# Down projections: the second column group takes every second slab by Strassen's scheme, with three more sets of side sums where x was

## The chip, the cores and the metric

The kernel runs on one core of one Trainium2 chip. The metric is the device time of one execution in microseconds (us). Before the change it is 2428.57 us, the median of three runs (2427.8 to 2428.59).

## What is computed

Two transformer blocks in a row on 256 tokens of width 2048, all in fp32. The part that the change touches is the last product of the feed-forward network, which occurs twice (once in each layer of the second block):

```python
D_FF = 5632
def swiglu(h, w_gate, w_up, w_down):
    return (jax.nn.silu(h @ w_gate) * (h @ w_up)) @ w_down
x = x + rmsnorm(swiglu(h, w_ffn_gate[l], w_ffn_up[l], w_ffn_down[l]), norm_ffn_post[l])   # l = 0, 1
```

So per layer a 256x5632 matrix g (gated activations) is multiplied by a 5632x2048 weight matrix. To keep fp32 accuracy every operand is split into a high part (rounded to the matmul type) and a low part (the rest), and each product is made of three matmuls: hi x hi, hi x lo, lo x hi.

## The kernel before

**Slabs.** Weights come in slabs of 1 MB: 128 partitions of 2048 floats, fetched as two DMAs of 512 KB by SyncE (L688, `fetch_part`). Each slab passes from SyncE (DMA into one of 5 ring places of `raw`) to ScalarE (`conv`, L1486: the high part into one of 4 places of `hi`), to VectorE (`conv`, L2098: the low part, in place), and to TensorE. A list `slabs`, made once, gives the order; every engine goes through it in that order. SyncE may fill a place when the slab five entries back is used, ScalarE may write `hi` when the slab four entries back is used (`slab_used`).

**A down projection** (`st_down[l]`) has two column groups g = 0 and 1 of 1024 output columns, and 22 slabs s = 0 to 21 in each. A slab holds two blocks of 128 rows by two halves of 512 columns. An ordinary slab is 2 token tiles x 2 column halves x 2 row blocks = 8 products, 24 matmuls of 128x512 (`product`, L808 to L810), accumulated in the four PSUM banks `acc`.

**Strassen's scheme** (`seven`, matmuls in L1248 to L1250). For the slabs named in `SEVEN[g]` the 2x2 by 2x2 block product is made of 7 products, so 21 matmuls. It takes sums of weight blocks and sums of activation blocks:
- The sums of weights (`weight_sums`, L2160 to L2163, VectorE, 4 operations) are made anew for each group. Three of them fill a ring place of their own; they are an entry `sums{s}` of `slabs` behind the slab, with a conversion of its own of 1536 columns (128x768 twice).
- The sums of activations ("side sums": `side_sums` on VectorE, L2236 to L2241, then `side_hi` on ScalarE, L1548, then `side_lo` on VectorE, L2246) are made once in group 0 and read again in group 1, so each needs 4 KB per partition of its own until group 1 has used it. There are five such sets, for slabs 3, 6, 9, 12, 15, and both groups use the scheme for just these five.
- Four of the seven products are accumulated in the PSUM banks `wk`. After the last such slab (15) VectorE combines them (`mix_products`, L2252 to L2256, in its order ahead of the conversion of slab 18) and adds them into `acc` (`mix_into_acc`, L2263 and L2266, ahead of the conversion of slab 19). TensorE waits for the first two additions ahead of slab 17's second token tile and for the other two ahead of slab 18's first one (`acc_loaded`, with `MIX_DONE` = 16).

On VectorE and ScalarE the order is one straight program: `conv_to(m)` goes through the slabs up to m, and `before(m)` holds what VectorE does ahead of the conversion of slab m. ScalarE does `side_hi` ahead of its conversion of the slab at which the side sums are made, so that conversion waits until VectorE has made the sums.

**x.** The residual x (16 KB per partition at `X0`) is stored to HBM earlier (`keep_x`), and its place is used for sums in the gate/up stage. SyncE fetches it back (`fetch_x`, L700, two DMAs of 1 MB) ahead of the weights of slab 3 of group 0, and VectorE waits for it (`x_fetched`) at the start of the down projection. Its first reader is `add_normed`, after the down projection.

Of the kernel before, what the change touches and what calls it, by code (L numbers as in the profile page):

```python
# [13 lines left out]
D = 2048  # L14
# [14 lines left out]
FG = FF // HALF  # L29
# [7 lines left out]
TAKEN_BELOW = -3.2e38  # L37
RING = 5
OWN_SLOT = 9
SEVEN = ((3, 6, 9, 12, 15), (3, 6, 9, 12, 15))  # L40
HI_SLOTS = 4
SLAB = 2048

# [53 lines left out]
def build(nc, t_in, out):  # L97
# [22 lines left out]
    m_a = at("m_a", [P, TT, 2 * D], A0)  # L120
    gain_a = at("gain_a", [P, D], A0 + 24)

    SIDES_AT = (A0 + 8, A0 + 12, A0 + 4, A0 + 20, S0 + 1)
    side = [at(f"side{i}", [P, 2, 4, P], kb) for i, kb in enumerate(SIDES_AT)]
    side_r = [at(f"side_r{i}", [P, 2, 4, P], kb, F32R) for i, kb in enumerate(SIDES_AT)]
    CHAINED = 2
# [207 lines left out]
    def sevens(m):  # L334

        st, g, s = slabs[m]
        return st_down.index(st) if st in st_down and s in SEVEN[g] else None
# [14 lines left out]

        return (FG - CHAINED) * l + g - CHAINED

    N_SIDES = len(SEVEN[0])
    DOWN_SIDES = [6 + l * (6 + 2 * N_SIDES) for l in range(2)]
    GU_SIDES = [l * (6 + 2 * N_SIDES) for l in range(2)]
    DOWN_HIS = [4 + l * (4 + N_SIDES) for l in range(2)]
# [295 lines left out]
    @block.sync  # L654
    def _(sp):
        def const(name, dst):
            a, w = CONSTS[name]
            sp.dma_start(dst, t_in["consts"][:, a:a + w]).then_inc(consts_in, 16)

        const("ident", ident[:])  # L660
        sp.dma_start(rows2[0:KT, :], t_in["c"][0].rearrange("(k p) -> k p", p=P)).then_inc(rows_in, 16)
        sp.dma_start(rows2[KT:2 * KT, :], t_in["hgrn_lb_logits"].rearrange("a (k p) -> (a k) p", p=P)).then_inc(rows_in, 16)

        def wait_summed(a):

            if a in PE_ADA:
                sp.wait_ge(ada_taken, PE_ADA.index(a) + 1)
            else:
                sp.wait_ge(ada_added, added(a + 1))

        def ada_fetch(a, landed):

            for part in range(2):
                src, dst = ada_part(a, part)
                sp.dma_start(dst, src).then_inc(landed, 16)

        for a in range(4):
            ada_fetch(a, raw_landed[1 + a])
        def fetch_part(slot, st, g, s, part, landed):

            src, (a, b), how = st.src(g, s, part)
            if how is None:
                dst = slot[:, a:b]
            elif how == "part":
                dst = slot.rearrange("p (k h n) -> p k h n", k=2, h=2)[:, :, part, :]
            else:
                dst = slot[:, a:b].rearrange("p (k n) -> p k n", n=how)
            sp.dma_start(dst, src).then_inc(landed, 16)  # L688

        def keep_x(l):  # L690

            sp.wait_ge(x_ready, 4 * l + 2)
            for t in range(TT):
                sp.dma_start(x_kept[:, t], x[:, t]).then_inc(stored, 16)

        def fetch_x(l):

            sp.wait_ge(slab_used, number[st_gu[l].name, FG - 1, "D"] + 1)
            for t in range(TT):
                sp.dma_start(x[:, t], x_kept[:, t]).then_inc(x_fetched, 16)  # L700

        def fetch_own(l, g):

            if g == CHAINED:
                sp.wait_ge(stored, 16 * TT * (l + 1))
                sp.wait_ge(x_squares, 8 + 4 * l)
                sp.wait_ge(h_ready, h_done((3, 6)[l]) + 8)
            else:
                sp.wait_ge(slab_used, number[st_gu[l].name, g - 1, "C"] + 1)
            for part in range(2):  # L710
                fetch_part(raw[:, OWN_SLOT], st_gu[l], g, 1, part, own_landed)

        for m, (st, g, s) in enumerate(RAWS):
            if st in st_gu:
                l = st_gu.index(st)
                if (g, s) == (0, 7):
                    keep_x(l)
                if s == 7 and g + 1 in OWN_GROUPS:
                    fetch_own(l, g + 1)
            if st in st_down and (g, s) == (0, 3):  # L720
                fetch_x(st_down.index(st))
            if isinstance(s, str):
                continue
            r = m % RING
            if m == 1:
                for a in range(4, N_QUARTER):
                    ada_fetch(a, early_landed[a - 4])
            if m == 2:
                ada_fetch(8, quarter_landed[0])
                sp.wait_ge(xn_ready, 1)  # L730
                ada_fetch(9, quarter_landed[1])
            if m == 3:
                sp.wait_ge(xn_ready, 2)
                ada_fetch(10, quarter_landed[2])
                sp.wait_ge(ada_added, added(7))
                ada_fetch(11, early_landed[2])
            if m == 4:
                sp.wait_ge(ada_added, added(8))
                ada_fetch(12, early_landed[3])
            if 1 <= m < RING:  # L740
                wait_summed(m - 1)
            elif m:
                sp.wait_ge(slab_used, LAST_USE[m - RING] + 1)
            for part in range(2):
                fetch_part(raw[:, r], st, g, s, part, raw_landed[r])

        for t in range(TT):
            for half in range(2):
                c = slice(half * GW, (half + 1) * GW)
                sp.wait_ge((x_half, x_ready)[half], 6 + t + 1)  # L750
                sp.dma_start(out[0, t * P:(t + 1) * P, c], x[:, t, c]).then_inc(stored, 16)
        sp.wait_ge(stored, 16 * 4 * TT)
# [3 lines left out]
    def _(pe):  # L756
# [479 lines left out]

        def seven(l, g, s):

            st, i = st_down[l], SEVEN[0].index(s)
            m = number[st.name, g, s]  # L1240
            k0, k1 = 2 * s, 2 * s + 1
            s1, s2, s3, s4 = ((side_r[i][:, 0, j, :], side_r[i][:, 1, j, :]) for j in range(4))

            def add(o, lhs, slab, q, first=False, last=False):

                c = slice(q * HALF, (q + 1) * HALF)
                w_hi, w_lo = hi[:, slab % HI_SLOTS, c], lo[:, place(*slabs[slab]), c]
                pe.matmul(o, lhs[0], w_hi, start=first, stop=False)  # L1248
                pe.matmul(o, lhs[0], w_lo, start=False, stop=False)
                return pe.matmul(o, lhs[1], w_hi, start=False, stop=last)  # L1250

            first, last = s == min(SEVEN[g]), s == max(SEVEN[g])
            pe.wait_ge(slab_split, m + 1)
            pe.wait_ge(g_ready, 2 * FG * (l + 1) if first else 2 * FG * l + s + 1)
            add(wk[:, 0, :], gt(k0, 0), m, 0, first, last)
            add(acc[:, 0, :], gt(k1, 0), m, 2)
            pe.wait_ge(side_made, DOWN_SIDES[l] + 2 * i + 2)
            add(acc[:, 1, :], s4, m, 3)
            add(wk[:, 3, :], s3, m, 1, first, last).then_inc(slab_used, 1)
            pe.wait_ge(slab_split, m + 2)  # L1260
            add(wk[:, 1, :], s1, m + 1, 0, first, last)
            add(wk[:, 2, :], s2, m + 1, 1, first, last)
            add(acc[:, 2, :], gt(k1, 1), m + 1, 2).then_inc(slab_used, 1)
# [199 lines left out]
    def _(act):  # L1463
# [43 lines left out]
        def conv_to(m):  # L1507

            while made[0] <= min(m, N_SLABS - 1):
                if sevens(made[0]) is not None and slabs[made[0]][1] == 0:  # L1510
                    side_hi(sevens(made[0]), SEVEN[0].index(slabs[made[0]][2]))
                conv(made[0])
                st, g, s = slabs[made[0]]
                if st in st_gu and g == CHAINED - 1 and s in (5, 6, 7):
                    l = st_gu.index(st)
                    if s > 5:
                        side_hi_pair(l, s - 6)
                    if s < 7:
                        tile_hi_pair(l, s - 5)
                made[0] += 1  # L1520
# [529 lines left out]
    def _(vec):  # L2050
# [63 lines left out]
        def conv_to(m):  # L2114

            while made[0] <= min(m, N_SLABS - 1):
                ada_to(ada_until(made[0]))
                before(made[0])
                conv(made[0])
                if sevens(made[0]) is not None and slabs[made[0]][1] == 0:  # L2120
                    side_lo(sevens(made[0]), SEVEN[0].index(slabs[made[0]][2]))
                made[0] += 1

        def before(m):
# [15 lines left out]
                    third_sum(l, g)  # L2140
            if st in st_down:
                l = st_down.index(st)
                if g == 0 and s in SEVEN[0]:
                    side_sums(l, SEVEN[0].index(s))
                if s in SEVEN[g]:
                    weight_sums(m)
                if s == MIX_DONE + 2:
# [79 lines left out]

        def side_sums(l, i):

            s, gu = SEVEN[0][i], st_gu[l]  # L2230
            a11, a21, a12, a22 = (side[i][:, 0, j, :] for j in range(4))
            s1, s2, s3, s4 = (side[i][:, 1, j, :] for j in range(4))
            flat = "p k t -> p (k t)"
# [599 lines left out]
        def ffn(l):  # L2833
# [31 lines left out]
            for g in range(FG):  # L2865
# [12 lines left out]
                else:  # L2878
                    conv_to(end + 4)
                post(g)  # L2880
            vec.wait_ge(x_fetched, 16 * TT * (l + 1))
            return m_evac(st_down[l], m_a, gain_a, (post_in, 16 * (l + 1)), 1 + 2 * l)

        skewed_turn(ffn(0), m_a, 1, 4, st_k)
        row_scale(3)
# [253 lines left out]
```

## Time and profile before

| | |
|---|---|
| median of three runs | 2428.57 us |
| profiled execution, own time | 2428.43 us |
| its span, first to last instruction | 2426.6 us |
| TensorE busy | 2384.8 us, 98% |
| VectorE busy | 1973.3 us, 81% |
| ScalarE busy | 1299.3 us, 54% |
| granted TensorE clock, mean | 0.996 |
| down projection of layer 0, about | 1100 to 1333 us of the span |
| down projection of layer 1, about | 2184 to 2418 us |

How to read it: the span is the time between the first and the last instruction of one profiled execution. Matmul durations overlap (they are pipelined), so the pace is read from one start to the next. A row "[1.25 <-PE acc L1250]" says that the engine was idle for 1.25 us before the instruction and that the matmuls of line 1250 ended the wait.

### The profile page before, as it was taken

How to read it: one execution, taken by the hardware profiler on the slowest of the kernel's cores; microseconds unless marked ns; L12 is line 12 of the kernel's file. 1: busy time of each engine (PE TensorE's matmuls, PEld its weight loads, DVE VectorE, ACT ScalarE, POOL GpSimd, SP SyncE). 2: the span in 40 equal slices, each digit the busy share in tenths (PEclk: the TensorE clock that was granted, in tenths of full speed). 3: DMA queues.
4: the chain of work that ended last, by engine and by line, in shares of the span. 5: the costliest groups of instructions: out<-in, count | busy, mean ns of one | idle time of the engine just before them, and what ended most of it. 6: DMA issues, size and time to landing. Idle time of an engine off the chain costs nothing.

```text
span 2426.6 us, 28811 instructions
## 1 busy us (share of the span) xinstructions
PE 2384.8 (98%) x11030; PEld 1979.5 (82%) x11030; DVE 1973.3 (81%) x2564; ACT 1299.3 (54%) x1703; POOL 99.0 (4%) x150
## 2 busy tenths in 40 slices
PE   5999999999999999999999999999999999999998
PEld 4888878888888888888888888888888888888887
DVE  6998988766889899897777768965699898988776
ACT  4757765445555555654444544554555555555443
POOL 0210000000000000000000212100000000000000
PEclk8999999999999999999999999999999999999999
DMA  9997665474566566566656655446666565565654
GB/s 383 360 385 246 240 208 171 166 262 167 192 208 208 191 208 196 186 199 215 229 188 205 196 196 193 160 142 203 218 210 200 188 212 188 195 222 189 224 191 156
DMA packets 190649, 515.46 MB, mean 212 GB/s; under 512 B 17920, under 2 KB 18208, under 8 KB 188208
## 3 DMA queue, kind: packets, MB, share of 16 engines
q1 hardware_dynamic: 178160, 465.31, 56.5%
q0 software_dynamic: 11824, 46.14, 5.1%
q8 instruction: 88, 1.44, 0.2%
q10 hardware_dynamic: 528, 2.16, 0.2%
q14 instruction: 49, 0.40, 0.0%
HBM read 507.26 MB, written 6.29 MB: 212 GB/s over the span
## 4 chain that ended last, share of the span: by engine, by line
PE 95%; DVE 2%; SPq 1%; DMA 0%; issue 0%; ACT 0%; DVEq 0%; ACTq 0%
PE acc L808 18%; PE acc L810 17%; PE acc L809 17%; PE acc L1276 4%; PE acc L1275 4%; PE acc L1277 4%; PE wk L1276 4%; PE wk L1275 4%; PE wk L1277 4%; PE acc L1317 1%; PE acc L1316 1%; PE acc L1318 1%; PE wk L1317 1%; PE wk L810 1%; PE wk L809 1%; PE wk L1316 1%
## 5 line engine op out<-in xcount | busy, mean ns | idle before, releaser
L2098 DVE TENSOR_TENSOR lo<-raw,hi 128x1024 fp32r<-128x1024 f32 (+2 forms) x428 | 486.8, 1188 | 110.2 <-ACT hi L1486 108.6
L1486 ACT ACTIVATE hi<-raw 128x1024 fp32r<-128x1024 f32 (+2 forms) x428 | 414.6, 1026 | 253.0 <-PE acc L810 122.1
L2100 DVE SCALAR_TENSOR_TENSOR lo<-raw,gcols,hi 128x1024 fp32r<-128x1024 f32 (+1 forms) x392 | 479.7, 1267 | 50.8 <-ACT hi L1486 48.3
L808 PE MATMUL acc<-hi,h 128*128 128x512 f32 x1312 | 519.4, 396 | 1.5 <-DVE lo L2098 0.5
L810 PE MATMUL acc<-hi,h 128*128 128x512 f32 x1312 | 511.7, 390 | 0.0
L809 PE MATMUL acc<-lo,h 128*128 128x512 f32 x1312 | 511.3, 390 | 0.0
L1486 ACT ACTIVATE hi<-raw,gcols 128x1024 fp32r<-128x1024 f32 (+1 forms) x392 | 416.6, 1124 | 140.4 <-PE acc L810 59.6
L808 PEld LDWEIGHTS acc<-hi,h 128*128 128x128 f32 x1312 | 246.8, 188 | 53.7 <-issue 2.7
L810 PEld LDWEIGHTS acc<-hi,h 128*128 128x128 f32 x1312 | 246.6, 188 | 52.3
L809 PEld LDWEIGHTS acc<-lo,h 128*128 128x128 f32 x1312 | 246.9, 188 | 49.1
L808 PE MATMUL acc<-hi,g_hi 128*128 128x512 f32 x544 | 211.9, 390 | 0.0
L810 PE MATMUL acc<-hi,g_lo 128*128 128x512 f32 x544 | 211.7, 389 | 0.0
L809 PE MATMUL acc<-lo,g_hi 128*128 128x512 f32 x544 | 211.6, 389 | 0.0
L1275 PE MATMUL acc<-hi,h 128*128 128x512 f32 x480 | 186.7, 389 | 0.0
L1276 PE MATMUL acc<-lo,h 128*128 128x512 f32 x480 | 186.7, 389 | 0.0
L1277 PE MATMUL acc<-hi,h 128*128 128x512 f32 x480 | 186.7, 389 | 0.0
L1275 PE MATMUL wk<-hi,h 128*128 128x512 f32 x400 | 155.6, 389 | 0.0
L1276 PE MATMUL wk<-lo,h 128*128 128x512 f32 x400 | 155.6, 389 | 0.0
L1277 PE MATMUL wk<-hi,h 128*128 128x512 f32 x400 | 155.6, 389 | 0.0
L2852 DVE STREAM_TRANSPOSE g_raw<-gated 32x256 f32<-32x256 f32 x320 | 139.4, 436 | 5.3
L810 PEld LDWEIGHTS acc<-hi,g_lo 128*128 128x128 f32 x544 | 102.1, 188 | 21.3
L809 PEld LDWEIGHTS acc<-lo,g_hi 128*128 128x128 f32 x544 | 102.1, 188 | 21.1
(445 smaller groups left out, 3403.8 us busy)
## 6 DMA issues: line engine op xcount, KB each, us to landing
raw<-in_w_ffn_gate SPq DMA_DIRECT2D x176, 512.0 KB, 3.8
raw<-in_w_ffn_up SPq DMA_DIRECT2D x176, 512.0 KB, 4.7
raw<-in_w_ffn_down SPq DMA_DIRECT2D x176, 512.0 KB, 4.7
raw<-in_w_in SPq DMA_DIRECT2D x144, 512.0 KB, 4.8
raw<-in_w_kv SPq DMA_DIRECT2D x64, 512.0 KB, 4.9
ada_raw<-in_ada_w POOLq DMA_DIRECT2D x38, 512.0 KB, 7.2
gate_raw<-in_ada_w POOLq DMA_DIRECT2D x32, 512.0 KB, 6.2
raw<-in_w_out SPq DMA_DIRECT2D x32, 512.0 KB, 4.8
```

The lines of the kernel that those rows point to most:

```text
L808: pe.matmul(o, l_hi, w_hi[:, c], start=first, stop=False, skip_group_check=loaded)
L809: pe.matmul(o, l_hi, w_lo[:, c], start=False, stop=False, skip_group_check=loaded)
L810: mm = pe.matmul(o, l_lo, w_hi[:, c], start=False, stop=last, skip_group_check=loaded)
L1275: pe.matmul(o, l_hi, w_hi, start=False, stop=False, skip_group_check=g >= CHAINED)
L1276: pe.matmul(o, l_hi, w_lo, start=False, stop=False, skip_group_check=g >= CHAINED)
L1277: mm = pe.matmul(o, l_lo, w_hi, start=False, stop=last, skip_group_check=g >= CHAINED)
L1316: pe.matmul(o, lhs[p][0], w_hi, start=first and p == 0, stop=False, skip_group_check=True)
L1317: pe.matmul(o, lhs[p][0], w_lo, start=False, stop=False, skip_group_check=True)
L1486: ins = act.activation(hi[:, m % HI_SLOTS, c], raw[:, r, c], ACT.Copy, scale=scale)
L2098: ins = vec.tensor_tensor(lo[:, r, c], raw[:, r, c], hi[:, m % HI_SLOTS, c], ALU.subtract)
L2100: ins = vec.scalar_tensor_tensor(out=lo[:, r, c], in0=raw[:, r, c], scalar=gcols[:, st.gain, k:k + 1], in1=hi[:, m % HI_SLOTS, c], op0=ALU ...
L2852: ins = vec.transpose(dst, src)
```

## The change

Group 0 uses the scheme for slabs 3, 7, 9, 13, 15 (still five), group 1 for 1, 3, 5, 7, 9, 11, 13, 15 (eight). The three sets of side sums for slabs 1, 5 and 11, which group 0 does not use, are made in group 0 at slabs 16, 17 and 20 (`LATE_SIDES`: place in the order, then slab), and lie at `X0`, `X0 + 4` and `X0 + 8` KB. So x is fetched back later: SyncE does it ahead of the weights of slab 17 of group 1, and waits for the sums of slab 11 of group 1 to be used. VectorE's wait for x moves behind the conversions of the down projection.

```diff
-SEVEN = ((3, 6, 9, 12, 15), (3, 6, 9, 12, 15))
+SEVEN = ((3, 7, 9, 13, 15), (1, 3, 5, 7, 9, 11, 13, 15))
+LATE_SIDES = {16: 1, 17: 5, 20: 11}
@@
-    SIDES_AT = (A0 + 8, A0 + 12, A0 + 4, A0 + 20, S0 + 1)
+    SIDES_AT = (A0 + 8, A0 + 12, A0 + 4, A0 + 20, S0 + 1, X0, X0 + 4, X0 + 8)
@@
-    N_SIDES = len(SEVEN[0])
+    SIDE_PAIRS = SEVEN[0] + tuple(LATE_SIDES.values())
+    N_SIDES = len(SIDE_PAIRS)
+
+    def sides_with(m):
+
+        st, g, s = slabs[m]
+        if st not in st_down or g:
+            return None
+        pair = s if s in SEVEN[0] else LATE_SIDES.get(s)
+        return None if pair is None else (st_down.index(st), SIDE_PAIRS.index(pair))
@@ fetch_x(l), SyncE
-            sp.wait_ge(slab_used, number[st_gu[l].name, FG - 1, "D"] + 1)
+            sp.wait_ge(slab_used, number[st_down[l].name, 1, "sums11"] + 1)
@@
-            if st in st_down and (g, s) == (0, 3):
+            if st in st_down and (g, s) == (1, 17):
                 fetch_x(st_down.index(st))
@@ seven(l, g, s), TensorE
-            st, i = st_down[l], SEVEN[0].index(s)
+            st, i = st_down[l], SIDE_PAIRS.index(s)
@@ conv_to, ScalarE
-                if sevens(made[0]) is not None and slabs[made[0]][1] == 0:
-                    side_hi(sevens(made[0]), SEVEN[0].index(slabs[made[0]][2]))
+                if sides_with(made[0]) is not None:
+                    side_hi(*sides_with(made[0]))
@@ conv_to, VectorE
-                if sevens(made[0]) is not None and slabs[made[0]][1] == 0:
-                    side_lo(sevens(made[0]), SEVEN[0].index(slabs[made[0]][2]))
+                if sides_with(made[0]) is not None:
+                    side_lo(*sides_with(made[0]))
@@ before(m), VectorE
-                if g == 0 and s in SEVEN[0]:
-                    side_sums(l, SEVEN[0].index(s))
+                if sides_with(m) is not None:
+                    side_sums(*sides_with(m))
@@ side_sums(l, i), VectorE
-            s, gu = SEVEN[0][i], st_gu[l]
+            s, gu = SIDE_PAIRS[i], st_gu[l]
@@ ffn(l), VectorE
+            evac_down = m_evac(st_down[l], m_a, gain_a, (post_in, 16 * (l + 1)), 1 + 2 * l)
             vec.wait_ge(x_fetched, 16 * TT * (l + 1))
-            return m_evac(st_down[l], m_a, gain_a, (post_in, 16 * (l + 1)), 1 + 2 * l)
+            return evac_down
```

## Rows read from the trace of the kernel before

**Rows 1.** The page: busy time of the engines.
```profile
PE 2384.8 (98%) x11030; PEld 1979.5 (82%) x11030; DVE 1973.3 (81%) x2564; ACT 1299.3 (54%) x1703; POOL 99.0 (4%) x150
```
**Rows 2.** Busy by stretch, layer 0, group 1: start:end, us, engines, clock, DMA share, GB/s.
```profile
1217.00:1312.00 95.00, 95.00 (x421) 78.69 (x420) 70.36 (x77) 46.38 (x51) 0.00 (x0) 1.00 0.59 199
```
**Rows 3.** Order of time, VectorE, layer 0, group 0, slabs 15 to 18.
```profile
1167.53 0.68 DVE L2236 TENSOR_TENSOR side<-g_hi,g_lo 128x512 f32<-128x512 f32 x1
...
1169.38 0.69 DVE L2160 TENSOR_TENSOR raw<-raw 128x512 f32<-128x512 f32 x1
...
1172.15 2.36 DVE L2098 TENSOR_TENSOR lo<-raw,hi 128x1024 fp32r<-128x1024 f32 x2
1174.43 0.68 DVE L2246 TENSOR_TENSOR side_r<-side,side_r 128x512 fp32r<-128x512 f32 x1
1175.04 4.09 DVE L2098 TENSOR_TENSOR lo<-raw,hi 128x768 fp32r<-128x768 f32 x4
...
1184.50 0.69 DVE L2252 COPY mixed<-wk 128x512 f32<-128x512 f32 x1 [1.25 <-PE acc L1250]
...
1190.40 1.29 DVE L2263 TENSOR_TENSOR acc<-acc,mixed 128x512 f32<-128x512 f32 x2
1192.66 1.30 DVE L2266 TENSOR_TENSOR acc<-acc,mixed 128x512 f32<-128x512 f32 x2 [0.97 <-PE acc L810]
```
**Rows 4.** Order of time, ScalarE, layer 0.
```profile
1111.52 1.07 ACT L1962 ACTIVATE g_hi<-wk 128x512 fp32r<-128x512 f32 x2
...
1208.86 2.01 ACT L1486 ACTIVATE hi<-raw 128x1024 fp32r<-128x1024 f32 x2 [5.97 <-DMA raw<-in_w_ffn_down]
...
1296.08 2.01 ACT L1486 ACTIVATE hi<-raw 128x1024 fp32r<-128x1024 f32 x2 [3.43 <-PE acc L810]
1301.35 2.01 ACT L1486 ACTIVATE hi<-raw 128x1024 fp32r<-128x1024 f32 x2 [3.27 <-DMA raw<-in_w_ffn_down]
```
**Rows 5.** Order of time, VectorE, layer 0, group 1.
```profile
1297.17 2.36 DVE L2098 TENSOR_TENSOR lo<-raw,hi 128x1024 fp32r<-128x1024 f32 x2 [2.43 <-ACT hi L1486]
1300.78 0.69 DVE L2252 COPY mixed<-wk 128x512 f32<-128x512 f32 x1 [1.25 <-PE acc L1250]
```
**Rows 6.** Order of time, SyncE's issues around `fetch_x`, layers 0 and 1.
```profile
1089.05 0.80 SPq L688 DMA_DIRECT2D raw<-in_w_ffn_down  x2
1089.90 0.43 SPq L700 DMA_DIRECT2D x<-x_kept  x1
1094.49 0.81 SPq L688 DMA_DIRECT2D raw<-in_w_ffn_down  x2
...
2178.89 0.81 SPq L688 DMA_DIRECT2D raw<-in_w_ffn_down  x2
```
**Rows 7.** DMA issues, windows 1094.3:1094.7, 1094.7:1095.5, 2178.5:2179.1, 2179.1:2180: median us to landing.
```profile
raw<-in_w_ffn_down SPq DMA_DIRECT2D x1, 512.0 KB, 6.7
raw<-in_w_ffn_down SPq DMA_DIRECT2D x2, 512.0 KB, 7.1
raw<-in_w_ffn_down SPq DMA_DIRECT2D x1, 512.0 KB, 7.0
raw<-in_w_ffn_down SPq DMA_DIRECT2D x2, 512.0 KB, 8.0
```
**Rows 8.** Order of time, TensorE, start of the kernel, around its two long waits.
```profile
27.49 3.67 PE L929 MATMUL wk<-ident,xn 128*128 128x128 f32 x16 [5.48 <-ACT xn L1613]
39.31 3.57 PE L943 MATMUL acc<-ones,gate 128*128 128x1 f32 x16 [8.15 <-DVE gate L2072]
46.05 0.78 PE L808 MATMUL acc<-hi,h 128*128 128x512 f32 x1
```
**Rows 9.** Busy by stretch; the granted clock is the third number from the end.
```profile
34.50:35.00 0.50, 0.00 (x0) 0.00 (x0) 0.50 (x1) 0.00 (x0) 0.00 (x0) 0.73 1.01 410
48.00:48.50 0.50, 0.50 (x3) 0.40 (x2) 0.50 (x2) 0.50 (x2) 0.00 (x0) 0.62 1.17 459
2420.50:2421.00 0.50, 0.00 (x0) 0.00 (x0) 0.42 (x3) 0.00 (x0) 0.00 (x0) 0.64 0.00 0
```

## The prediction

> **What bounds the kernel now.** First the busy times: TensorE works 2384.8 of 2426.6 us [rows 1]. Then the busy times by stretch: in group 1 of layer 0's down projection TensorE has no idle time at all, VectorE works 70.4 of 95.0 us, the clock is at its full 2.4 GHz level and the DMA engines carry 199 GB/s [rows 2]. So only matmuls count here, as long as VectorE's conversions come in time. How much time they have to spare is read in the order of time. The pace: slab 15's matmuls end at 1184.46, and the first half of slab 17 ends at 1192.62 (both 0.04 before the VectorE row that they release) [rows 3]; between them lie 24 + 12 matmuls, so 8.16 / 36 = 0.2267 us each. An ordinary slab takes 24 x 0.2267 = 5.44 us, a Strassen slab 21 x 0.2267 = 4.76 us, of which 2.72 on its first 12 matmuls.
>
> One place is tight already. TensorE may begin slab 17's second token tile only when the first two of the mixed products are in `acc`. That time is 1192.62 in group 0, and VectorE has them there at 1190.40 + 1.29 = 1191.69 [rows 3]. The margin is 0.93 us. VectorE's work from the start of mixing to that point, the "mix chain", is 1191.69 - 1184.50 = 7.19 us: five mixing operations, slab 18's conversion, two additions. In group 1 the same chain starts at 1300.78, when slab 15 is used [rows 5]. Whatever delays its start by more than 0.93 us stops TensorE by the excess.
>
> **The gain.** Three more Strassen slabs per layer, two layers, 3 matmuls each: 18 x 0.2267 = 4.1 us. The matmuls of both are of the same shape, and in group 0 the count stays five. This is 0.17% of the time, so even whole it would lie inside what a measurement of this kernel can tell (about 0.2%, 4.9 us).
>
> **Late side sums, group 0 (the costly part).** VectorE's prices [rows 3]: side sums 1.8 (1167.53 to 1169.38 with a trace of a wait), sums of weights 2.77 (1169.38 to 1172.15), a slab's conversion 2.28 (to 1174.43), side low part 0.61, conversion of the weight sums 4.09 - 2.28 = 1.81. A Strassen slab of group 0 thus costs VectorE 9.27, an ordinary one 2.28. TensorE's slab ends, back from 1184.46 (the five Strassen slabs give the same sum): 14 at 1179.70, 13 at 1174.26, 12 at 1169.50, 8 at 1148.42. Slab 12 can be fetched when slab 8 is used; a transfer issued at a slab's end reaches ScalarE 5.3 later (issued when 14 is used, 1295.98 from 1300.74 less 4.76; ScalarE starts at 1301.35 [rows 4]), and VectorE's low part follows ScalarE's start by 1.09 (1296.08 to 1297.17) [rows 4, 5]. So slab 12's conversion starts on VectorE at 1154.8. From there it has 12, 13, 14, 15 without a gap: 2 x (2.28 + 9.27) = 23.1, done at 1177.9. TensorE needs the last of it at 1179.70 + 2.72 = 1182.4, no harm. Before the change VectorE was idle next; now it must do, ahead of mixing, all of this twice (slabs 16 and 17): side sums 1.8; ScalarE's side part and the first half of its conversion, which waited for the sums, 0.04 + 0.53 (half of the two 512-column copies' 1.07) [rows 4] + 1.09 = 1.66; conversion 2.28; side low part 0.61. That is 6.35 each, 12.7 together. Slab 16 is ready at 1183.6 (needed 1184.46), slab 17 at 1190.0 (needed 1189.90). Mixing starts at 1177.9 + 12.7 = 1190.6 and not at 1184.50, and the chain is through at 1197.8. TensorE wanted it at 1192.62: **it stands 5.2 us, twice, 10.3 us.** Bounds: slab 15's transfer, issued when slab 11 is used at 1164.06, lands at 1169.4, where VectorE comes to it at 1170.4, so VectorE can't be over 1.0 earlier: 4.2 to 5.5 each. The third late set (slab 20) comes when VectorE has caught up: after the chain it needs 1.3 + 2.28 + 6.35 = 9.9 to 1207.7, and TensorE needs slab 20 over 10 us after 1197.8 + 2.7. Nothing.
>
> **The boundary of the groups.** Slab 1 now wants its weight sums before its conversion. Its weights land at 1208.86 [rows 4]; 2.77 + 2.36 later, 1214.0, it is done, and the four evacuations that follow take place at their old times. TensorE ends group 0 at 1217.1 and slab 0 at 1222.6, its weight sums are needed at 1225.3 and done by 1220.5. Nothing.
>
> **Alternating slabs, group 1.** Per pair VectorE has 2.28 + 2.77 + 2.28 + 1.81 = 9.14 us of work in TensorE's 5.44 + 4.76 = 10.20. Let E be the end of a Strassen slab. The two next transfers are issued at E - 2.04 and E; the first lands at E + 3.3, so VectorE has that ordinary slab at E + 6.6 (needed at E + 10.2), the next Strassen slab at E + 11.7 (needed at E + 15.6), its sums at E + 13.5 (needed at E + 18.4). A margin of 3.6 us or more each time, and it repeats. I take 0; the other bound, if every pair lost what a 10% slower VectorE would miss, is still 0 (10.05 is under 10.20).
>
> **x fetched at slab 17 of group 1.** Its wait is met, so the 2 MB go out directly behind slab 16's weights at E - 1.2 (E is now the end of slab 13, 1290.5 on the old time), ahead of slab 17's weights in the one queue. The same sequence stands in the trace at group 0's start: weights at 1089.05, x at 1089.90, next weights at 1094.49 [rows 6]. Their first half landed 6.7 after its issue and the pair's median is 7.1, so the second at 1094.9 + 7.5 = 1102.4, 13.4 after 1089.05; in layer 1 7.0, 8.0, so 9.0: 2188.3, 14.9 after 2173.45, one slab before 2178.89 [rows 6, 7]. There nothing waited on it. At its new place slab 17 lands at E + 11.4 (layer 0) or E + 12.9 (layer 1), its conversion ends 0.04 + 1.09 + 2.28 = 3.4 later, and mixing, queued behind it on VectorE, starts at E + 14.8 or E + 16.3 and not at E + 10.24. The excess over 0.93: **TensorE stands 3.6 and 5.1 us, together 8.7.** From below: if the queue lost its idle start and all 4 MB landed at E + 10, each is 2.2. What x's move gives at the old place is nothing, as TensorE doesn't wait there.
>
> **The clock.** The row: the wait of 5.48 us left the clock at full level; the one of 8.15 us, from 31.2 to 39.3, saw it fall to the 1.2 GHz level at 34.7, and it fell again at 2420.6, 3 us after the last matmul [rows 8, 9]. After 46.05 dense matmuls ran at the low level until 48.4, so a fall costs about half of 2.3, 1.2 us. Standing times of 4 to 5 us lie between: 0 to 4 falls, 0 to 4.8 us; I take one, 1.2 us. The Trainium skill ("TensorE: Matmul & The Clock Gate", "Why this matters for your kernels") warns that an idle gap between bursts of matmuls in mid-kernel sets the clock back to half. By that rule each of the four would fall, 4.8 and not 1.2 us; the 5.48 us wait speaks against it, the two falls for it.
>
> **Sum**, against the profiled execution's own 2428.43 us (0.1 off the median of 2428.57): -4.1 + 10.3 + 8.7 + 1.2 = +16.1, so **2444.5 us**.
>
> **The rivals.**
> 1. *x's transfer does no harm* (slab 17's weights overtake it or the two queue faster), only the late side sums stop TensorE: -4.1 + 10.3 + 0 to 1.2: 2435 us. For it: a 1 MB slab alone lands in 5.3. Against: the 6.7 to 9.0 of rows 7. 12%.
> 2. *Every stop costs the clock, and more than 1.2*, since it stays low for longer behind a stop in dense work: 4 x 1.2 to 2.0: -4.1 + 19 + 6.5 = 2450 us. 13%.
> 3. *The mix chain doesn't bind*, the end on the other side: if VectorE is through with the two late sets within 0.93 us of the old start of mixing (it would have to be 4 us earlier at slab 15, or TensorE's wait to be met otherwise) and slab 17 is early, only the 18 matmuls count: 2424.3 us, not slower. For it: VectorE has idle waits in every period of the old order. Against: those waits are used up by the denser order, add up above. 5%.
> 4. *The alternation starves TensorE*: transfers of two slabs in a row land over 3.6 us later than computed, and each of seven periods loses some 0.5 us: 2448 us. Against: 199 GB/s [rows 2] of engines that carry over 400 elsewhere [rows 9]. 5%.
>
> Forecast 65%. The range holds the bounds: low, -4.1 + 8.4 + 4.4 and no fall is 2437, and it reaches down to rival 1's lower half at 2434; high, -4.1 + 11 + 10.2 + 4.8 is 2450. Slower by over 0.2% (above 2433.4) takes the forecast, rivals 1 but for a small part, 2 and 4: 91%. Within 0.2%: rival 3 and that part, 8%. Faster by over 0.2% needs more than the whole gain: 1%.
>
> **What would show it.** In the changed kernel TensorE waits four times on the additions into `acc` (VectorE, L2263's counterpart) at slab 17's second token tile: about 5 us in each group 0, 3.5 to 5 in each group 1; VectorE's first mixing operation is no longer released by TensorE but follows its own work (group 0) or ScalarE's conversion of slab 17, which waits for weights (group 1); TensorE has 18 matmuls less and no other new wait. The forecast is wrong if those waits are short, if TensorE waits for conversions inside the alternation, or if the granted clock falls behind each stop.

## The result

The changed kernel takes 2453.61 us (median of four runs, 2450.97 to 2457.02), the kernel before 2428.58: ratio 1.0104, 95% interval 1.0092 to 1.0117, or 25 us slower. The forecast was 2444.5 (range 2434 to 2450): the right direction and the right places, but too little.

The page of the changed kernel, its first row, answers to [rows 1]. Eighteen matmuls are gone, the span is 2455.2 us (+28.6; the profiled execution, with 2457.02 us of its own, is the slowest of the four), and TensorE is busy longer:

```profile
PE 2392.5 (97%) x11012; PEld 1981.5 (81%) x11012; DVE 2013.8 (82%) x2636; ACT 1310.1 (53%) x1721; POOL 99.0 (4%) x150
```

Two stretches of layer 0 (group 0 from slab 2 to its end, and the first 110 us of group 1, which ends at 1348.7), with columns as in [rows 2]: TensorE now idles 6.0 and 5.2 us, and the granted clock has a mean of 0.97 where it was 1.00.

```profile
1112.00:1225.00 113.00, 107.03 (x462) 87.50 (x461) 94.06 (x128) 53.19 (x64) 0.53 (x1) 0.97 0.57 196
1225.00:1335.00 110.00, 104.82 (x451) 85.98 (x450) 88.43 (x97) 54.71 (x60) 0.00 (x0) 0.97 0.61 216
```

TensorE's waits over the whole changed kernel (total us, times, longest); the same view of before has nothing in the first row's place and 0.5 in the second's, a wait outside the down projections that is among the six here too:

```profile
PE acc L819 <- DVE acc L2274: 17.9, 4, 4.8
...
PE acc L819 <- DVE lo L2109: 3.4, 6, 1.0
```

L2274 is the first pair of additions into `acc`. So there are four stops there, as forecast. VectorE in layer 0's group 0, slabs 16 to 18 (answers to [rows 3]; start, us, instruction):

```profile
1178.48 0.68 DVE L2247 TENSOR_TENSOR side<-g_hi,g_lo 128x512 f32<-128x512 f32 x1
...
1182.00 2.36 DVE L2109 TENSOR_TENSOR lo<-raw,hi 128x1024 fp32r<-128x1024 f32 x2 [1.65 <-ACT hi L1497]
...
1188.39 2.36 DVE L2109 TENSOR_TENSOR lo<-raw,hi 128x1024 fp32r<-128x1024 f32 x2 [1.65 <-ACT hi L1497]
...
1191.27 0.69 DVE L2263 COPY mixed<-wk 128x512 f32<-128x512 f32 x1
...
1197.17 1.29 DVE L2274 TENSOR_TENSOR acc<-acc,mixed 128x512 f32<-128x512 f32 x2
```

The two late sets, each with its 1.65 us of waiting for ScalarE, push mixing from 1184.50 to 1191.27 (computed 1190.6); no releaser stands behind it, VectorE was simply busy. What TensorE does behind the stop:

```profile
1198.61 0.77 PE L819 MATMUL acc<-hi,g_hi 128*128 128x512 f32 x1 [4.77 <-DVE acc L2274]
1199.17 0.63 PE L820 MATMUL acc<-lo,g_hi 128*128 128x512 f32 x1
1199.60 0.63 PE L821 MATMUL acc<-hi,g_lo 128*128 128x512 f32 x1
```

and the stretches around it, with the granted clock third from the end:

```profile
1196.00:1197.00 1.00, 0.00 (x0) 0.00 (x0) 1.00 (x2) 0.00 (x0) 0.00 (x0) 0.53 0.00 0
...
1202.00:1203.00 1.00, 1.00 (x4) 0.78 (x4) 0.93 (x3) 0.00 (x0) 0.00 (x0) 0.56 0.00 0
```

Here the granted clock falls to its 1.2 GHz level while TensorE stands still, and the matmuls behind the stop start 0.43 us apart, not 0.23, until 1202.9. Group 1 of layer 0, around x's transfer (SyncE, ScalarE, VectorE):

```profile
1296.33 0.91 SPq L711 DMA_DIRECT2D x<-x_kept  x2
```
```profile
1302.50 2.01 ACT L1497 ACTIVATE hi<-raw 128x1024 fp32r<-128x1024 f32 x2 [3.95 <-DMA raw<-in_w_ffn_down]
1309.91 2.01 ACT L1497 ACTIVATE hi<-raw 128x1024 fp32r<-128x1024 f32 x2 [5.39 <-DMA raw<-in_w_ffn_down]
```
```profile
1311.00 2.36 DVE L2109 TENSOR_TENSOR lo<-raw,hi 128x1024 fp32r<-128x1024 f32 x2 [5.04 <-ACT hi L1497]
1313.28 0.68 DVE L2263 COPY mixed<-wk 128x512 f32<-128x512 f32 x1
```

Slab 17's weights, queued behind x and asked for about when slab 13 has been used (its end, E, is 1296.6), reach ScalarE at 1309.9, and mixing starts right behind their conversion.

**The account of the +28.6 us.** It adds up, over the two down projections, what the starts of two matmuls in a row lie apart beyond 0.2267 us. It holds for the profiled execution; the median one is 3.4 us faster, so against the forecast it lacks 9.1 us and not 12.5.

| part | forecast | measured |
|---|---|---|
| 18 matmuls less | -4.1 | -4.1 |
| group 0's stops, two layers | 10.3 | 12.1 (at the additions 4.93 and 4.94; ahead of slabs 16 and 17 0.8 + 0.9 and 0.5) |
| group 1's stops, two layers | 8.7 | 10.7 (at the additions 4.34 and 4.34; ahead of slab 17 1.3 and 0.8) |
| matmuls at the low clock | 1.2 | 10.1 (42 whole ones at 0.43 us: 8.4; the first behind each stop and those in which the clock came back: 1.7) |
| sum | 16.1 | 28.8 |

### The profile page after: what moved, and what is told of

Read it like the earlier page. It is cut to its first block, busy times and chain, and to the rows that moved or that the text cites. A ratio compares the mean times of both kernels' runs of the same rounds, so it can differ in the third digit from the quotient of the medians.

```text
span 2455.2 us, 28887 instructions
## 1 busy us (share of the span) xinstructions
PE 2392.5 (97%) x11012; PEld 1981.5 (81%) x11012; DVE 2013.8 (82%) x2636; ACT 1310.1 (53%) x1721; POOL 99.0 (4%) x150
## 4 chain that ended last, share of the span: by engine, by line
PE 90%; DVE 6%; DMA 2%; issue 1%; ACT 1%; SPq 0%; DVEq 0%; ACTq 0%
PE acc L819 16%; PE acc L821 16%; PE acc L820 16%; PE acc L1287 4%; PE acc L1286 4%; PE acc L1288 4%; PE wk L1287 4%; PE wk L1286 4%; PE wk L1288 4%; DVE lo L2109 2%; DMA raw<-in_w_ffn_down 1%; PE acc L1327 1%; PE acc L1328 1%; PE acc L1329 1%; PE wk L821 1%; PE wk L1328 1%
## 5 line engine op out<-in xcount | busy, mean ns | idle before, releaser
L2109 DVE TENSOR_TENSOR lo<-raw,hi 128x1024 fp32r<-128x1024 f32 (+2 forms) x440 | 498.8, 1182 | 112.2 <-ACT hi L1497 110.4
L1497 ACT ACTIVATE hi<-raw 128x1024 fp32r<-128x1024 f32 (+2 forms) x440 | 422.8, 1020 | 240.2 <-DMA raw<-in_w_ffn_down 68.0
L819 PE MATMUL acc<-hi,g_hi 128*128 128x512 f32 x496 | 198.4, 400 | 20.8 <-DVE acc L2274 17.9
L820 PE MATMUL acc<-lo,g_hi 128*128 128x512 f32 x496 | 196.9, 397 | 0.0
L821 PE MATMUL acc<-hi,g_lo 128*128 128x512 f32 x496 | 196.5, 396 | 0.0
L819 PEld LDWEIGHTS acc<-hi,g_hi 128*128 128x128 f32 x496 | 95.7, 193 | 44.4 <-DVE acc L2274 19.5
L1515 ACT ACTIVATE hi<-t 128x1024 fp32r<-128x1024 f32 x72 | 74.3, 1055 | 81.3 <-DVE t L2191 64.8
```

The costliest lines, as they stand in the source:

```text
L819: pe.matmul(o, l_hi, w_hi[:, c], start=first, stop=False, skip_group_check=loaded)
L820: pe.matmul(o, l_hi, w_lo[:, c], start=False, stop=False, skip_group_check=loaded)
L821: mm = pe.matmul(o, l_lo, w_hi[:, c], start=False, stop=last, skip_group_check=loaded)
L1497: ins = act.activation(hi[:, m % HI_SLOTS, c], raw[:, r, c], ACT.Copy, scale=scale)
L1515: act.activation(dst, part_source(st, g, kind, q), ACT.Copy).then_inc(hi_made, 2 if part == "D" else 1)
L2109: ins = vec.tensor_tensor(lo[:, r, c], raw[:, r, c], hi[:, m % HI_SLOTS, c], ALU.subtract)
```

## The experiments

The theory behind them was that three things made the time: the late sets ahead of mixing, x ahead of slab 17's weights, and a fall of the clock at each stop, while the alternation of group 1 costs nothing. The main rival was that the denser order itself costs (VectorE's load, DMA in bursts). The eight kernels ran on chips that measured the kernel before at 2428.24 us (e1 to e4) and 2428.62 us (e5 to e8).

**e1: x one period earlier.**

```diff
-            if st in st_down and (g, s) == (1, 17):
+            if st in st_down and (g, s) == (1, 16):
```

> The changed kernel with x fetched ahead of slab 16's weights of group 1 instead of slab 17's (one period of the queue earlier, when slab 11's sums are used). Theory: both waits of group 1 on the additions into acc (4.3 us each) and the waits ahead of slab 17 (1.2 and 0.7 us) go, and with them the two falls of the clock behind them (about 2.4 and 2.9 us): about 15.5 us off the changed kernel's 2453.6, so 2438 us. Rival: x's 2 MB hurt wherever they stand in the dense alternation; then a wait of about the same length shows at slab 15 or 16 and the time stays within 4 us of 2453.

Measured: 2442.85 us, ratio 1.0060 (1.0046 to 1.0074). TensorE's waits in layer 0's group 1:

```profile
PE acc L819 <- DVE acc L2274: 1.2, 1, 1.2
PE acc L819 <- DVE lo L2109: 0.4, 1, 0.4
```

The stops of 4.3 us are down to 1.4 and 1.1 from start to start, with no fall of the clock behind them; 10.8 of the expected 15.5 us are back. Not all of the wait goes: x's 2 MB still make slabs 16 and 17 late, and mixing starts 2.9 and 1.9 us behind the end of slab 15. So it is x's place, but "all gone" was wrong.

From profile to profile (spans of 2455.2 and 2439.8 us) the difference is 15.4 us, and only 13.0 of it lie in group 1. The rest lies in group 0, which the edit does not touch: its two stops at the additions are 4.9 us long in both, but the matmuls at the low clock behind them cost 1.5 and 1.7 us here and 2.1 and 2.5 in the changed kernel's profile. A stop of the same length does not always cost the same, and the expectation had taken the stops of a slow execution from the median time.

**e2: the late sets in VectorE's idle stretches.** Each set of side sums keeps its place in memory by its slab; only the order in which they are made changes.

```diff
-LATE_SIDES = {16: 1, 17: 5, 20: 11}
+LATE_SIDES = {5: 1, 11: 5, 20: 11}
-    SIDES_AT = (A0 + 8, A0 + 12, A0 + 4, A0 + 20, S0 + 1, X0, X0 + 4, X0 + 8)
+    SIDES_AT = (A0 + 8, X0, A0 + 12, A0 + 4, X0 + 4, A0 + 20, S0 + 1, X0 + 8)
-    SIDE_PAIRS = SEVEN[0] + tuple(LATE_SIDES.values())
+    SIDE_PAIRS = (3, 1, 7, 9, 5, 13, 15, 11)
```

> The changed kernel with the three extra sets of side sums made at slabs 5, 11 and 20 of group 0 (in VectorE's idle stretches between Strassen slabs) and not at 16, 17 and 20; x as in the changed kernel. Theory: the waits of group 0 go (4.9 us twice at the additions, 0.7 + 0.8 and 0.4 ahead of slabs 16 and 17) with two falls of the clock (2.0 and 2.4 us): about 16.3 us off 2453.6, so 2437 us; group 1 keeps its stops. Rival: the whole VectorE load of group 0 is what makes mixing late, not the place of the late sets; then the chain stays 3 us or more late and the time above 2446.

Measured: 2437.75 us, ratio 1.0041 (1.0027 to 1.0055). From slab 2 to the end of layer 0's group 0 TensorE has no wait at all; in the two down projections these are left, all in group 1:

```profile
PE acc L819 <- DVE acc L2274: 8.3, 2, 4.2
PE acc L819 <- DVE lo L2109: 1.6, 2, 1.1
```

With the same work on VectorE in group 0, at other slabs, the stops are gone: the place counted, not the load.

**e3: both.** The edits of e1 and e2 together.

> Both edits: side sums at 5, 11, 20 and x ahead of slab 16. Theory: no stop of TensorE is left in the down projections, only the 18 matmuls fewer count: 2428.6 - 4.1 = 2424.5 us, ratio 0.998. Rival: the alternation in group 1 costs something by itself (matmul pace, waits for conversions): 2428 us or more.

Measured: 2427.53 us, ratio 0.9996 (0.9987 to 1.0005), so no difference that can be told. Left are, over both down projections:

```profile
PE acc L819 <- DVE acc L2274: 1.7, 2, 1.2
PE acc L819 <- DVE lo L2109: 0.5, 1, 0.5
```

The expectation of 2424.5 failed by what e1 had already shown: x ahead of slab 16 is not free.

**e4: x's place by itself**, in the kernel before.

```diff
-            if st in st_down and (g, s) == (0, 3):
+            if st in st_down and (g, s) == (1, 17):
```

(with VectorE's wait for x behind the conversions, as in the change)

> The kernel before with x alone moved to slab 17 of group 1, the Strassen slabs as they were. There slab 16's and 17's weights are asked for 5.44 us apart and not 2.04. Theory: slab 17 lands 13.4 to 14.9 us behind the first issue as in the row of group 0's start, so mixing starts 1.1 to 2.6 us late, less the margin of 0.93: stops of 0.2 and 1.7 us, too short for the clock to fall: about 2430.5 us. Rival: x's move costs what it cost in the changed kernel (4.3 us and more with a fall of the clock behind it, in each layer) whatever the order: about 2444 us.

Measured: 2431.31 us, ratio 1.0013 (1.0004 to 1.0022). The additions are late by little:

```profile
PE acc L808 <- DVE acc L2263: 3.0, 2, 1.5
```

From start to start they are 1.7 and 1.6 us (0.2 and 1.7 expected), with the clock at 1.00. With slab 16's and 17's transfers a whole slab apart x's move costs 3 us; in the alternating order, with 2.04 us between them, it costs two stops of 4.3 us, waits ahead of slab 17, and the clock. That the shorter distance is the reason is argued from the prediction's times; no run changes it alone.

**e5 and e6: nothing but stops.** The kernel before, with 4 or 7 more copies of one PSUM bank on VectorE ahead of mixing:

```diff
+            for _ in range(4):        # e6: 7
+                step(vec.tensor_copy(b[3][:], wk[:, 3, :]))
             step(vec.tensor_copy(b[0][:], wk[:, 0, :]))
```

> The kernel before with four more copies (0.72 us each) on VectorE ahead of mixing, in both groups and both layers; their results are overwritten. Theory: each of the four chains is 2.9 us late, less the margin of 0.93: four stops of 2.0 us, and as they are short the granted clock stays at its full level: 2428.4 + 7.9 = 2436.3 us. Rival: any stop of TensorE in dense work sets the clock to half behind it, at about 2 us each: 2444 us.

> The same with seven copies: chains 5.1 us late, four stops of 4.1 us, 16.6 us in all, with nothing else of the change in the kernel. Theory: most of these stops bring a fall of the clock with 1 to 3 us at half rate behind each, so 2428.4 + 16.6 + 4 to 10 = 2449 to 2455 us, and two stops of unequal cost by when they fall. Rival: the time beyond the stops in the changed kernel belongs to its denser order and not to the stops: 2445 us and a clock at its full level.

Measured: e5 2442.30 us, ratio 1.0058 (1.0044 to 1.0071), e6 2455.66 us, ratio 1.0112 (1.0098 to 1.0126). TensorE's waits in each:

```profile
PE acc L808 <- DVE acc L2265: 8.5, 4, 2.1
```
```profile
PE acc L808 <- DVE acc L2265: 17.2, 4, 4.3
```

e6 has a loss like the changed kernel's (27.0 us) without any of its change: four stops of 4.45 us from start to start (17.8 us), and 10.3 us more behind them, of which 44 whole matmuls at the low clock are 8.8. The rival that gave the extra time to the denser order is out. e5's expectation failed, and it is the instructive one. Its stops are 2.3 us where 2.0 were expected (9.1 in all and not 7.9), and in three of the four the clock fell as well. The matmuls behind its second stop:

```profile
1312.63 0.52 PE L808 MATMUL acc<-hi,g_hi 128*128 128x512 f32 x1 [2.12 <-DVE acc L2265]
1312.95 0.63 PE L809 MATMUL acc<-lo,g_hi 128*128 128x512 f32 x1
1313.38 0.63 PE L810 MATMUL acc<-hi,g_lo 128*128 128x512 f32 x1
```

and the granted clock behind the first and the second (third number from the end):

```profile
1194.00:1198.00 4.00, 4.00 (x18) 3.29 (x19) 4.00 (x5) 0.94 (x1) 0.00 (x0) 1.00 0.03 5
...
1313.00:1316.00 3.00, 3.00 (x9) 2.32 (x8) 3.00 (x5) 0.00 (x0) 0.00 (x0) 0.50 0.00 0
```

These are two stops of the same length, one with a fall and one without. Of the 6.0 us beyond the expectation, 22 matmuls at the low rate are 4.4 us and the longer stops 1.2. In all three falls the clock fell only when TensorE was working again, 0.1 to 0.9 us behind its restart. The latest is the one at the third stop, where the first three matmuls still start 0.2 to 0.3 us apart and only those from 2285.91 on 0.43:

```profile
2284.82 0.47 PE L808 MATMUL acc<-hi,g_hi 128*128 128x512 f32 x1 [2.12 <-DVE acc L2265]
...
2285.91 0.63 PE L809 MATMUL acc<-lo,g_hi 128*128 128x512 f32 x1
```

In e1, e3, e4 and e7 there are eight stops of 0.7 to 1.8 us at the additions, none with a fall behind it.

**e7: one late set ahead of mixing.**

```diff
-LATE_SIDES = {16: 1, 17: 5, 20: 11}
+LATE_SIDES = {16: 1, 20: 5, 21: 11}
```

> The changed kernel with one late set ahead of mixing (slab 16) and the others at 20 and 21. Theory: the chain of group 0 starts one set, 4.1 us (side sums 1.8, the handing over to ScalarE 1.7, side low part 0.6), earlier, so its stop falls from 4.9 to about 0.9 us or less and the waits ahead of slab 17 go; no fall of the clock in group 0: 2453.6 - 2 x 4.1 - 1.2 - 2 x 2.2 = 2440 us. Rival: the stop belongs to slab 15's late end and stays over 3 us: 2448 us.

Measured: 2442.44 us, ratio 1.0059 (1.0045 to 1.0073). The stops of group 0 are 1.8 and 1.3 us from start to start, with the clock at 1.00 behind both; group 1 keeps its 4.4 and 4.3. With one late set and not two ahead of mixing, each stop is 3.2 to 3.6 us shorter, and no fall comes with it. It was 2.4 us slower than expected: the stops are 0.4 to 0.9 longer, and the wait ahead of slab 16 in layer 0 is 1.2 us where the changed kernel had 0.7.

**e8: a version that is better than both.** e2's side sums, and x behind all that mixing waits for:

```diff
-            if st in st_down and (g, s) == (1, 17):
+            if st in st_down and (g, s) == (1, 20):
```

> Side sums at slabs 5, 11, 20 and x ahead of slab 20's weights, behind everything that mixing waits for. Theory: the stops of 0.7 and 1.9 us that were left in group 1 with x ahead of 16 go as well and the 18 matmuls come out whole: 2424.3 us, ratio 0.998. Rival: x now lands too late for the additions behind the down projection or pushes the next stage's weights: a new wait of 1 us or more at the end of group 1 and 2427 us or more.

Measured: 2424.82 us (median of eleven runs, 2423.72 to 2426.88), ratio 0.9986, interval 0.9977 to 0.9995. TensorE's one wait in the down projections (layer 0, group 0), and the stretch of group 1 of [rows 2]:

```profile
PE acc L819 <- DVE acc L2274: 0.4, 1, 0.4
```
```profile
1217.00:1312.00 95.00, 95.00 (x421) 78.69 (x420) 81.12 (x90) 48.88 (x55) 0.00 (x0) 1.00 0.66 233
```

VectorE works 81.1 of 95 us instead of 70.4, the DMA engines carry 233 GB/s instead of 199, and TensorE has no idle time and starts the same 421 matmuls as before. The alternation costs nothing that can be seen. The medians lie 3.8 us apart, where 18 matmuls are worth 4.1; the interval allows 1.2 to 5.6 us.

## Why the prediction was wrong, step by step

- **The gain, -4.1 us: right.** e8 brings 3.8 (1.2 to 5.6), with 0.4 us of waiting left.
- **Late side sums, group 0: right in mechanism, 1.8 us short.** Mixing at 1191.27 against 1190.6; in all 6.6 and 5.4 us of stop against 5.2 each, some of it already ahead of slabs 16 and 17, which I had 0.9 us early and 0.1 late. VectorE ran 0.7 late from slab 12 on (its conversion there began at 1155.58, not 1154.8). e2 and e7 show that it is these sets and their place.
- **x at slab 17: right in mechanism, 2.0 us short.** 5.6 and 5.1 us against 3.6 and 5.1. In layer 0 the weights reached ScalarE 13.3 us after E, where I had 11.4; in layer 1 the forecast held. e1 and e8 show that the cause is x's place ahead of the weights that mixing waits for.
- **The clock, "I take one, 1.2 us": this step failed.** All four stops had a fall, and each cost 2.1 to 3.0 us, 10.1 together: 8.9 of the 12.5 us missed. Two errors lie in it. The number of falls was guessed from two early waits [rows 8, 9], and the one of 5.48 us was taken as one without a fall, since the record's clock stands at 1.00 there. The pace of the matmuls says otherwise: the sixteen transposes of L929 behind that wait took 3.67 us (the first of rows 8), and the sixteen that follow at 42.75, where the record has 0.50, took the same. These are the kernel before, its transposes and the clock at both places:

```profile
42.75 3.65 PE L929 MATMUL wk<-ident,xn 128*128 128x128 f32 x16
```
```profile
28.00:30.00 2.00, 2.00 (x11) 2.00 (x10) 1.90 (x2) 2.00 (x4) 0.00 (x0) 1.00 1.05 408
...
42.00:44.00 2.00, 2.00 (x11) 2.00 (x11) 0.53 (x3) 2.00 (x5) 0.00 (x0) 0.50 1.03 410
```

  e3's profile shows it with dense matmuls. Its clock reads 1.00 from the start to the end of the down projections, but two of the first matmuls of 128x512 start 0.42 us apart, the pace of the low level:

```profile
47.36 0.63 PE L820 MATMUL acc<-lo,h 128*128 128x512 f32 x1
47.78 0.45 PE L821 MATMUL acc<-hi,h 128*128 128x512 f32 x1
```
```profile
46.00:48.00 2.00, 2.00 (x9) 1.81 (x8) 1.99 (x2) 2.00 (x5) 0.00 (x0) 1.00 1.05 411
```

  So a clock of 1.00 at the start of a profile is no evidence, and the 5.48 us wait gave no ground for stops without a fall. The second error is the price. It was taken from a fall whose low stretch lay mostly under a wait and small matmuls; behind these stops dense matmuls ran at the low level for 4 to 6 us, not 2.3, and so they do in e6 with nothing else in the kernel. The sentence on the Trainium skill's rule had the right count, and rival 2 (2450 us, 13%) the better price. "The granted clock falls behind each stop" was among the prediction's own signs of being wrong.
- **The boundary and the alternation at nothing: right** (e8). Rival 4's 2448 us counts its seven periods of 0.5 us in one layer only; with both it would be 2451.5.

## What to carry to other kernels

When TensorE has no idle time, price a new stop of more than 2 us with the clock on top: the 17 falls of these runs cost 1.5 to 3.0 us each, and in the changed kernel stops of 4.3 to 4.9 us cost 6.8 to 7.5. Before a stretch of the profile is taken as evidence for a clock level, compare the pace of its matmuls with that of equal ones elsewhere. When work is added to an in-order engine, its place counts more than its amount: the same three sets cost 16 us (2453.6 against e2's 2437.8) with two of them ahead of a chain that TensorE waits for, and no wait in group 0 at slabs 5, 11 and 20. The same holds for a large transfer in a queue that also carries weights: put it behind the last weights that a chain with little slack needs (slab 20 here, not 17 or 16).

## What was not expected of the hardware

Stops of TensorE of 2.3 us in otherwise dense work had a fall of the clock in three of four cases (e5), two stops of equal length in one execution differed in that, and the three falls came when TensorE was already working again. Over all profiles, none of the eight stops of 0.7 to 1.8 us at the additions had a fall, and all fourteen of 4.3 to 4.9 us had one. What decides at 2.3 us, and what makes one fall cost 1.5 us and another 3.0, is left open; no run here separates it. The record's clock of 1.00 at the kernel's start does not agree with the pace of the matmuls there (0.42 us apart at 1.00 in e3).
